# The first stage of a hybrid decoder block, reordered: copies and two sums by accumulating transfers, meta rows last, masks early

## The reference, cut to what matters

```python
meta = meta_tokens                                   # (16, 1024)
z = concatenate([meta, x], axis=1)                   # (1, 16 + 1024, 1024)
h = z * rsqrt(mean(z * z, axis=-1) + 1e-6) * norm_w  # RMS norm, row by row
p = h @ w_in + b_in                                  # w_in is (1024, 8192)
q, f, v, g, u, pool_gate, m_hg, m_pool = split(p)
# HGRN2 recurrence on q, f, v, chunk by chunk; causal pooling of u; two gates;
# three more 1024x1024 products; final RMS norm; the 16 meta rows are dropped
```

## Time and profile before

| | |
|---|---|
| median of 3 runs | 1032.16 us (1032.06 to 1032.34) |
| profiled execution, its own time | 1032.56 us |
| its span, first to last instruction | 1030.8 us |
| PE busy | 1011.9 us (98%) |
| DVE busy | 815.3 us (79%) |
| ACT busy | 512.5 us (50%) |
| POOL busy | 100.0 us (10%) |

### The profile page before, as it was taken

One profiled execution on the slowest core, in us unless ns is written; L12 is line 12 of the kernel. 1 busy time (PEld: TensorE's weight loads), 2 busy tenths in 40 slices (PEclk: granted clock), 3 DMA queues, 4 the chain that ended last, 5 costly groups with the idle time before them and its releaser, 6 DMA issues.

```text
span 1030.8 us, 18610 instructions
## 1 busy us (share of the span) xinstructions
PE 1011.9 (98%) x7216; PEld 829.2 (80%) x7216; DVE 815.3 (79%) x1344; ACT 512.5 (50%) x862; POOL 100.0 (10%) x162
## 2 busy tenths in 40 slices
PE   7999999999999999999999999999999999999997
PEld 7767888888888888878888888888887888788886
DVE  7988787868787878777676768885687879988985
ACT  7754636363635354544353435344447536435665
POOL 6200000101010101010101010102111011000130
PEclk9999999999999999999999999999999999999999
DMA  7221110202020202122213122227883393668374
GB/s 280 52 82 63 41 64 23 83 21 84 21 84 22 82 23 66 40 70 86 82 42 113 42 93 62 93 72 259 294 295 98 119 356 132 202 217 303 93 155 145
DMA packets 46856, 117.20 MB, mean 114 GB/s; under 512 B 4880, under 2 KB 13072, under 8 KB 46768
## 3 DMA queue, kind: packets, MB, share of 16 engines
q1 hardware_dynamic: 23680, 70.33, 20.7%
q0 software_dynamic: 8976, 26.26, 8.0%
q10 hardware_dynamic: 14112, 19.41, 5.5%
HBM read 86.62 MB, written 29.36 MB: 113 GB/s over the span
## 4 chain that ended last, share of the span: by engine, by line
PE 89%; DVE 7%; issue 1%; ACT 1%; DMA 1%; POOL 0%; DVEq 0%; SPq 0%; ACTq 0%
PE acc L1653 74%; PE levels L1708 2%; PE miscs L1741 1%; PE miscs L1742 1%; PE miscs L1730 1%; DVE r_lo L2541 1%; PE acc L1595 1%; PE levels L1653 1%; PE miscs L1532 1%; PE levels L1532 1%; DVE w_lo L1952 1%; PE levels L1714 1%; PE miscs L1748 1%; PE miscs L1721 1%; PE miscs L1683 1%
## 5 line engine op out<-in xcount | busy, mean ns | idle before, releaser
L1653 PE MATMUL acc<-r_hi,w_hi 128*128 128x512 f32 x1196 | 329.9, 397 | 3.0 <-ACT second L996 1.1
L1653 PE MATMUL acc<-r_lo,w_hi 128*128 128x512 f32 x1196 | 327.4, 392 | 0.5 <-DVE r_lo L2541 0.3
L1653 PE MATMUL acc<-r_hi,w_lo 128*128 128x512 f32 x1196 | 320.8, 390 | 0.5 <-DVE w_lo L1952 0.5
L1653 PEld LDWEIGHTS acc<-r_lo,w_hi 128*128 128x128 f32 x1196 | 222.3, 188 | 53.3 <-issue 4.9
L1653 PEld LDWEIGHTS acc<-r_hi,w_lo 128*128 128x128 f32 x1196 | 224.3, 188 | 48.8 <-DVE w_lo L1952 1.0
L1653 PEld LDWEIGHTS acc<-r_hi,w_hi 128*128 128x128 f32 x1196 | 217.9, 188 | 49.4 <-DVE zq L2046 1.6
L906 ACT ACTIVATE w_hi<-sum 128x512 fp32r<-128x512 f32 x164 | 102.9, 628 | 164.8 <-DVE sum L1985 82.4
L1952 DVE TENSOR_TENSOR w_lo<-sum,w_hi 128x512 fp32r<-128x512 f32 x164 | 111.9, 686 | 50.9 <-ACT w_hi L906 50.2
L1952 DVE TENSOR_TENSOR w_lo<-raws,w_hi 128x512 fp32r<-128x512 f32 x120 | 82.0, 685 | 49.6 <-ACT w_hi L906 49.6
L906 ACT ACTIVATE w_hi<-raws 128x512 fp32r<-128x512 f32 x120 | 74.7, 624 | 27.0 <-PE acc L1653 25.1
L996 ACT ACTIVATE second<-acc,bias 128x512 f32<-128x512 f32 x31 | 21.2, 685 | 59.8 <-PE acc L1653 59.7
(11 more groups left out here) (325 smaller groups left out, 1317.0 us busy)
## 6 DMA issues: line engine op xcount, KB each, us to landing
raws<-in_wstream SPq DMA_DIRECT2D x80, 512.0 KB, 3.6
xin<-in_x SPq DMA_DIRECT2D x8, 512.0 KB, 6.6
a_spill<-gt POOLq DMA_DIRECT2D x16, 256.0 KB, 3.4
c_spill<-pg POOLq DMA_DIRECT2D x16, 256.0 KB, 2.7
comb<-in_wstream ACTq DMA_DIRECT2D x8, 512.0 KB, 6.6
comb_spill<-comb ACTq DMA_DIRECT2D x8, 512.0 KB, 4.8
smh_spill<-zq POOLq DMA_DIRECT2D x16, 256.0 KB, 4.4
stage<-a_spill ACTq DMA_DIRECT2D x4, 1024.0 KB, 10.4
```

Of the source, the lines that this page charges most:

```text
L1653: ins = pe.matmul(bank[:, :], weights, moving, start=n == 0 and i in (0, 1, y_first), stop=n == 3 * KH - 1, skip_group_check=True)
```

## The change

- **Loads.** SP loads tiles 1 and 2, then the row of norm weights (which ACT's queue issued first of all before), then tiles 3 and 4, the weights and tiles 5 to 8, and then the meta rows and `raw_early`. The meta rows have buffers of their own (`x_meta`, `h_meta`); tile 5 takes a buffer that is free and waits for nothing.
- **Tiles.** Tiles 1 to 4 go first through every engine, the meta tile last of nine (`turn`). The first tiles use other PSUM banks. `first_tile` is split into `b11_high` and `b21_high`; its third copy and `b11_copy` are gone.
- **Whole copies.** `begin_whole(n)` on SP copies the finished `r_hi` of B11 (n = 0) and of B21 (n = 1) into a whole buffer, 1 MB each, and `make_whole(n)` on POOL accumulates `r_lo` onto it, 1 MB each.
- **V7 and V4.** `v7_sum` and `v4_sum` on DVE are gone. `make_v7` and `make_v4` on POOL are accumulating transfers of 1 MB each. V7's and V4's `high` wait for them.
- **PE.** Products (0,0) and (0,1) are whole; tiles 5 to 8 are transposed in the halves of (1,0) and (1,1). `meta_product(0)` stands ahead of (0,2), the transposition of the meta tile ahead of (1,3), `meta_turn(0)` in (0,4). 25 warming matmuls take the place of 38.
- **Masks.** POOL makes 13 of the 14 mask instructions ahead of `x_rstd(4)` and spreads the masks right behind it.
- **Side work.** The softmax parts move back: on ACT the Exp stands behind `meta_tile`, which stands behind `v5_high(1)`; on DVE the last part stands behind `low(16)`.
- Two semaphores of the last stage are merged into others; no instruction of an engine changes there.

```diff
-WARM_UP = (16, 4, 4, 4, 4)
+WARM_UP = ((1, 12), (2, 3), (3, 4), (4, 2))
...
+            def begin_whole(n):
+                if n:
+                    sp.wait_ge(S["whole_begun"], 16)
+                    sp.wait_ge(S["h_copied"], 4)
+                    dst, src = b21_whole, r_hi[R_B21]
+                else:
+                    sp.wait_ge(S["h_hi"], 4)
+                    dst, src = b11_whole, r_hi[R_B11]
+                sp.dma_start(dst[:, :, :], src[:, :, :].bitcast(F32)).then_inc(S["whole_begun"], 16)
+
-            sp.dma_start(xin[0][0:META, :], meta[:, :]).then_inc(x_loaded[0], 16)
             load_x(1)
             load_x(2)
+            sp.dma_start(nw[:, :], norm_w[0:1, :].to_broadcast([P, D])).then_inc(S["norm_row_loaded"], 16)
             load_x(3)
             load_x(4)
             load_raw(0)
+            load_raw(1)
             load_x(5)
-            load_raw(2)
             load_x(6)
             load_x(7)
-            load_raw(1)
+            load_raw(2)
+            load_x(8)
+            sp.dma_start(x_meta[0:META, :], meta[:, :]).then_inc(S["early_loaded"], 16)
             sp.dma_start(raw_early[:, :], wstream[3]).then_inc(S["early_loaded"], 16)
-            load_x(8)
...
             begin_third(0)
+            begin_whole(0)
+            begin_whole(1)
             begin_third(1)
...
+            def make_whole(n):
+                pool.wait_ge(S["whole_begun"], 16 * n + 16)
+                if n:
+                    pool.wait_ge(S["whole_made"], 16)
+                    pool.wait_ge(S["h_lo"], 4)
+                    dst, src = b21_whole, r_lo[R_B21]
+                else:
+                    pool.wait_ge(S["b11_lo"], 4)
+                    dst, src = b11_whole, r_lo[R_B11]
+                pool.dma_start(dst[:, :, :], src[:, :, :].bitcast(F32), accum_op=ALU.add).then_inc(S["whole_made"], 16)
+
+            def make_v7():
+                pool.wait_ge(S["v5_made"], 4)
+                pool.wait_ge(S["h_copied"], CHUNKS)
+                pool.dma_start(r_lo_f[R_V7][:, :, :], b22_whole[:, :, :], accum_op=ALU.add).then_inc(S["v7_made"], 16)
+
+            def make_v4():
+                pool.wait_ge(S["v6_made"], 2)
+                pool.wait_ge(S["whole_made"], 32)
+                pool.dma_start(b21_whole[:, :, :], v6_whole[:, :, :], accum_op=ALU.add).then_inc(S["v4_made"], 16)
...
 POOL's list, as it is after:
             memset; keep odd; keep_from(1, 2, 0); keep_from(2, 4, 0)
             x_rstd(1)
             keep level0; keep_from(3, 5, 4)
             x_rstd(2)
             keep_from(3, 6, 0); keep_from(4, 7, 0)
             keep odd; keep_to(1, 2, 1); keep level0
             x_rstd(3)
             keep_to(2, 4, 3); keep_to(3, 5, 7); keep_to(3, 6, 3)
             x_rstd(4)
             keep_to(4, 7, 15); spread_masks()
             x_rstd(5); x_rstd(6); x_rstd(7)
             make_whole(0); x_rstd(8); make_third(0); make_whole(1); x_rstd(0); make_third(1); make_v7(); make_v4()
...
 ACT's list, as it is after, from the first tiles on:
             square_x(1); square_x(2); square_x(3); b11_high(1); square_x(4); b21_high(1); b11_high(2); high(0)
             b11_high(3); b11_high(4); b21_high(2); b21_high(3); b21_high(4); high(1); square_x(5); high(2)
             square_x(6); square_x(7); copy_first(0); square_x(8); high(3); second_tile(5); second_tile(6)
             second_tile(7); high(4); second_tile(8); square_x(0); high(5); copy_first(1); v5_high(0); high(6)
             copy_early_fifth(0); v5_high(1); meta_tile(); Exp; Sigmoid (table load); high(7); v6_high(0)
             copy_early_fifth(1); meta_copy(0); v6_high(1); high(8); high(9); high(10); v7_high(0); v7_high(1)
...
 DVE's list, as it is after:
             x_mean(1); x_mean(2); h_row(1); h_row(2); x_mean(3); h_row(3); x_mean(4); b11_low(1); h_row(4)
             b11_low(2); b11_low(3); low(0); b11_low(4); b21_low(1); low(1); b21_low(2); b21_low(3); b21_low(4)
             x_mean(5); early_sum(0, S1); x_mean(6); h_row(5); x_mean(7); h_row(6); low(2); add_11(0); x_mean(8)
             h_row(7); early_sum(0, S2); h_row(8); low(3); early_sum(0, S4); early_sum(1, S1); b22_low(5)
             early_sum(1, S2); b22_low(6); low(4); b22_low(7); b22_low(8); early_sum(1, S4); x_mean(0); v5_sum(5)
             v5_sum(6); low(5); v5_sum(7); v5_sum(8); h_row(0); v5_low(0); low(6); v5_low(1); (softmax, first part)
             v6_sum(0); low(7); v6_sum(1); v6_low(0); low(8); v6_low(1); low(9); low(10); v7_low(0); v7_low(1)
...
-            for i in range(5):
-                keep_warm(WARM_UP[i])
+            for i, n in WARM_UP:
+                keep_warm(n)
                 h_transposes(i)
-            keep_warm(6)
+            keep_warm(2)
             product(0, 0)
-            half(0, 1, 0)
+            product(0, 1)
+            half(1, 0, 0)
             h_transposes(5)
-            half(0, 1, 1)
+            half(1, 0, 1)
             h_transposes(6)
-            half(1, 0, 0)
+            half(1, 1, 0)
             h_transposes(7)
-            half(1, 0, 1)
+            half(1, 1, 1)
             h_transposes(8)
-            for p, i in ORDER[3:2 * PRODUCTS]:
+            for p, i in ORDER[4:2 * PRODUCTS]:
+                if (p, i) == (0, 2):
+                    meta_product(0)
+                elif (p, i) == (1, 3):
+                    h_transposes(0)
                 product(p, i)
```

More of the change, by code:

```diff
@@ L386, in hybrid_block @@
         VM, KM, KVM = slice(128, 256), slice(256, 384), slice(384, 512)
-        h_banks = ((misc[0], misc[1]), (lev, small))
+        h_banks = {i: (acc[2], acc[1]) if i == 3 else (acc[3], lev) if i == 4
+                   else (lev, small) if i in (1, 6, 8) else (misc[0], misc[1]) for i in range(CHUNKS + 1)}
         final_banks = (acc[2], acc[3])
@@ L788, in _ @@
             make_third(0)
+            make_whole(1)
+            x_rstd(0)
             make_third(1)
-            spread_masks()
+            make_v7()
+            make_v4()
             pool.wait_ge(S["masks_spread"], 1)
@@ L1191, in gate_sigmoid @@
                 act.activation(gs[:, :], gt[:, HALF:SEQ], ACT.Sigmoid).then_inc(S["gs_made"], 1)
[L1194 removed]
             square_x(1)
             square_x(2)
[L1197 removed]
             square_x(3)
[L1199 to L1201 removed]
+            b11_high(1)
             square_x(4)
[L1203 removed]
+            b21_high(1)
+            b11_high(2)
+            high(0)
+            b11_high(3)
+            b11_high(4)
+            b21_high(2)
+            b21_high(3)
+            b21_high(4)
+            high(1)
             square_x(5)
[L1205 to L1208 removed]
+            high(2)
             square_x(6)
             square_x(7)
[L1211 to L1213 removed]
             act.wait_ge(S["params_loaded"], 48)
             copy_first(0)
+            square_x(8)
+            high(3)
+            second_tile(5)
             second_tile(6)
[L1217 removed]
             second_tile(7)
+            high(4)
             second_tile(8)
[L1220 to L1221 removed]
+            square_x(0)
+            high(5)
             copy_first(1)
[L1223 removed]
             v5_high(0)
@@ L1227, in _ @@
             v5_high(1)
+            meta_tile()
+            act.wait_ge(S["lb_shifted"], 1)
+            act.activation(lexp[:, :, :], lexp[:, :, :], ACT.Exp).then_inc(S["lb_exp"], 1)
             act.activation(o_ms[:, 0:1], minus_half[:, 0:1], ACT.Sigmoid)
             high(7)
+            v6_high(0)
             copy_early_fifth(1)
-            v6_high(0)
+            meta_copy(0)
             v6_high(1)
@@ L2250, in gated_o @@
                     dve.tensor_tensor(g, misc[q][:, :], g, ALU.mult).then_inc(S["a_made"], 1)
-            x_mean(0)
-            dve.wait_ge(S["norm_row_loaded"], 16)
+            x_mean(1)
+            x_mean(2)
+            dve.wait_ge(S["norm_row_loaded"], 16)
+            h_row(1)
+            h_row(2)
+            x_mean(3)
+            h_row(3)
+            x_mean(4)
+            b11_low(1)
+            h_row(4)
+            b11_low(2)
+            b11_low(3)
+            low(0)
+            b11_low(4)
+            b21_low(1)
+            low(1)
+            b21_low(2)
+            b21_low(3)
+            b21_low(4)
+            x_mean(5)
+            early_sum(0, S1)
+            x_mean(6)
+            h_row(5)
+            x_mean(7)
+            h_row(6)
+            low(2)
+            add_11(0)
+            x_mean(8)
+            h_row(7)
+            early_sum(0, S2)
+            h_row(8)
+            low(3)
+            early_sum(0, S4)
+            early_sum(1, S1)
+            b22_low(5)
+            early_sum(1, S2)
+            b22_low(6)
+            low(4)
+            b22_low(7)
+            b22_low(8)
+            early_sum(1, S4)
+            x_mean(0)
+            v5_sum(5)
+            v5_sum(6)
+            low(5)
+            v5_sum(7)
+            v5_sum(8)
             h_row(0)
-            x_mean(1)
-            h_row(1)
-            x_mean(2)
+            v5_low(0)
```

(2 more changed lines are left out.)

279 lines of the change are left out of this document (109 added, 170 removed).

## The result

The changed kernel takes 1043.26 us (median of 4 runs, 1042.34 to 1046.01), the kernel before on the same chip 1032.25 (4 runs, 1032.06 to 1033.31). The ratio is 1.0102, interval 1.009 to 1.0114. The kernel became slower by 1.0%; my 1033.7 and the whole of my range, 1028.8 to 1036.8, are too low. The profiled execution took 1042.34 us with a span of 1040.6, against 1030.8 before: the trace shows 9.8 us of the 11.0.

The account below looks back on a forecast made before the run. PE bounds the kernel, busy 98%, with about 20 us not useful. Start -3.1, before (0,5) +2.3, (0,3) -0.7, meta rows and hand-offs +0.6, +2.5, +1.0, +1.95, then -3.0: net +1.5, median 1033.7 us, range 1028.8 to 1036.8.

Parts of the forecast that it names:

- The start: Stretch up to the first product: POOL's masks set the pace, (0,0) starts at 18.7, 3.1 us earlier; bounds 17 and 20.
- To (0,5): PE from (0,0) to (0,5): idles 3.0 us for DVE's b22_low, (0,5) starts at 36.9 instead of 37.67.
- To the meta tile: (0,5), (1,5) and (0,3) on PE: v5_low(1) is late, so (0,3) ends at 45.6.
- The transfers: 1 MB accumulations at 8.6 us each: B11 whole at 34.6, 3.0 ahead of need; nothing added.
- The first hand-off: Ahead of (1,3): high(7) stands behind meta_tile on ACT, PE idles 2.5 us and starts (1,3) at 48.7.
- The sum: Net of all terms +1.5 us: pair 2 starts at 71.3, profiled execution 1034.1, median 1033.7.
- low clock: Rival, 12%: first products start at the low clock for 6 us and lose 3.0, all but 1.9 hidden: 1035.6.
- The second hand-off: Ahead of (0,2): high(8) stands behind meta_copy(0) and v6_high(1) on ACT, PE waits 1.95 us.
- I find no wait in this part: From (0,2) to pair 2: 16.9 us instead of 19.93; earlier waits of 1.11 and 0.54 go.
- Hand-offs hidden: Rival, 20%: the two waits ahead of (1,3) and (0,2) cost nothing; price -4.5 us, 1029.2.
- Late transfers: Rival, 10%: V4 lands after (0,6) wants it, from about 10 us per MB; at 11, 3 us late: 1036.7.

Follow-up runs that it names:

- e7: e3 with nine POOL mask instructions moved from between the four powers to behind x_rstd(4): 1031.79 us, ratio 0.9986.
- e6: e3 with the transpositions of tiles 7 and 8 half a product earlier, second_tile(8) and the four b22_low also earlier: 1034.47 us, ratio 1.0008.
- e11: e7 with the cover of e6 and begin_whole(0) issued ahead of the meta rows, raw_early and the first third: 1032.02 us, ratio 0.9982.
- e1: Changed kernel with copy_early_fifth(1), which empties the bank of (1,5), moved ahead of meta_tile on ACT: 1039.78 us, ratio 1.0058.
- e4: Changed kernel with sixteen products of the identity on PE between the meta transposition and (1,3): 1038.82 us, ratio 1.0053.
- e9: e7 with high(11) moved ahead of meta_place(0, 0) on ACT: 1032.12 us, ratio 0.9987.
- e3: Changed kernel with high(7), copy_early_fifth(1) ahead of meta_tile; v6_high, high(8) ahead of meta_copy(0); Exp, table load behind high(9): 1033.16 us, ratio 1.0003.
- e8: e3 with the V7 and V4 sums on DVE again instead of accumulating transfers: 1034.64 us, ratio 1.0015.
- e12: e11 with high(11) early and nine products of the identity in PE's wait near 460 us: 1030.92 us, ratio 0.9978.
- e5: e3 with twelve products of the identity on PE ahead of (0,5): 1034.55 us, ratio 1.0005.
- e10: e7 with 18 products of the identity on PE in the wait near 460 us: 1032.98 us, ratio 0.9997.

## Why the prediction was wrong

By its own steps:

**The start** was right to 0.5 us: (0,0) at 18.21 for 18.7. POOL set the pace: five masks took 2.84 us around DVE's rows, and `h_row(3)` waited 1.98 us for the power. e7 shows it from the other side.

**To (0,5)** was right to 0.9 us: 35.99 for 36.9, with an idle of 2.51 for 3.0, put down to `b22_low`.

**To the meta tile**: the transposition starts at 46.50 for 45.6. The term is (0,3). It starts at 42.74, and it waits for V5 and so for the whole B11. e6 and e11 show that the transfers set it.

**The transfers** were mis-sized. I took 8.6 us for 1 MB and a copy landed by 26; the copy landed at 27.3, 9.2 us after its issue behind the loads, and the accumulation issued at 27.56 took 10.5, with the copy of B21 and a third's accumulation (issued at 29.06) under way beside it. The four accumulations took 7.6 to 10.8 us. B11 was whole at 38.1, not at 34.6: my slack of 3.0 us was in truth a wait of 1.62. That V7 and V4 are in time held: PE never waited for them. The estimate of 4.4 us for 1 MB by the Trainium skill, "DMA: Bandwidth & Descriptors", section "Anatomy of one DMA", is still further off for accumulations: each of the four took at least 7.6.

**The first hand-off is the step that failed**, "PE idles 2.5 us and starts (1,3) at 48.7". The chain that I added up is right to 0.2 us: e1, where it alone is left, shows 2.66. But I asked only which weights (1,3) needs. It also needs its bank, which (1,5) had filled. On ACT its copy stands behind `high(7)` and `v6_high(0)`, 1.6 us more: 4.09.

**The clock.** The sum had no term for it: (1,3) was to take 2.7 us. My rival *low clock* had the right price, half of the time spent at the low level, and the wrong place: it looked at the first products, which ran at full speed (1.16 per four at 18.21). The drop came where PE stood still longest, ahead of (1,3), and cost 2.0 us there (4.92 us up to the meta product, where e1 and e4 take 2.91 and 2.94; my 2.7 left out 0.2 for the restart). e4 shows that it goes when PE is kept busy in the same wait. A second one near 460 us cost 1.5. Whether the drop at (1,3) would have come without the slip on the bank is open: behind the wait of 2.66 us that was left in e1 the clock stayed full in the one execution profiled.

**The second hand-off** was right: 2.01 for 1.95, and the meta product 1.0.

**"I find no wait in this part"** was wrong: 18.92 us from (0,2) to pair 2 for 16.9. Of the 1.11 and 0.54 that were to go only the 1.11 went. Two waits of 0.54 and 0.53 stayed, and each restart costs 0.1 to 0.2 more (1.19 instead of 1.07 for the first four, and what lies before). Part is the third hand-off (0.5, e9), which has the same form as the two that I had found: an instruction that waits for PE, with the high part of the next weights behind it. The rest is the low part and `st` on DVE, of before's kind.

The sum, in starts of pair 2: predicted 71.3, measured 78.17. The 6.9 us are 0.9 for (0,3), 1.6 for the bank, 2.0 for the clock, 0.3 for restarts around (1,3) and at the second hand-off, and 2.0 behind it. With 1.4 near 460 us this makes 8.3; the profiled execution was 1042.34 against 1034.1 in my sum, 8.2.

**The rivals.** *Hand-offs hidden* was refuted as told of this kernel, but e3 is its mechanism made true by moving five steps: 1033.16, ratio 1.0003. Its price of 4.5 us was too low: hiding them brought pair 2 forward by 8.3 us, the bank's 1.6 and the clock's 2.0 among them. *Low clock* did not happen ahead of (0,0) in the profile of the change, but in e8's it did and delayed (0,0) by 0.6 us. *Late transfers* named the wrong transfer: V4 was in time, the first one was not.

**What stays open.** Whether a wait of 2.4 to 2.8 us drops the clock differs from one execution to the next, and single executions of one kernel differ by 1 to 5 us. The mean granted clock of each execution goes with its time in part. In e9 the three fastest (1030.1 to 1030.7) had 0.998 to 0.999, the two slowest (1034.1 and 1035.1) 0.994 and 0.993; in e4, with 0.999 in all, the range is 1.2 us. But in e3 the slowest execution (1036.39) had 0.997 and one of 1033.03 had 0.996, so the clock is not all of it. The mean also counts what costs nothing: in e12's profile, with a mean of 0.998, the only low stretch is at 1025 to 1029 us, and the last matmul ends at 1023. Nor is the spread of the change's making: the kernel before took 1031.76 to 1035.36 in the 31 executions beside e5 to e8, at 0.996 to 0.999. What else differs between executions I did not find out.

## What to carry to other kernels

When a step is moved to stand directly ahead of a product, list everything that the product waits for, its bank as well as its operands, and follow each of them back through its engine's queue: every instruction between the one that waits for PE and the one that PE waits for is paid in full. Then put these instructions ahead of the wait; here moving five steps of ACT's list was worth 10 us. And where PE stands still for as long as the 4.1 us here, add to the idle time the price of the lower clock behind it, or give PE something harmless to do in the gap, but less than the gap holds. That paid in the gap of 4.1 us (e4); in those of about 2.5 us (e5, e10) the median gained nothing.
